# A shifted table of taps for the state-space stage: eight strided transfers, or one from a copy in DRAM

## The reference

```python
bu = einsum('blgc,gpc->blgp', u, bb)             # input to the states
s  = associative_scan(_complex_affine_combine, (a, bu), axis=1)
y  = einsum('blgp,gcp->blgc', s_re, c_re) - einsum('blgp,gcp->blgc', s_im, c_im) + d_skip * u
```

## Time and profile before

| | |
|---|---|
| median of 3 runs | 2849.48 us (2845.38 to 2862.76) |
| profiled execution | 2856.6 us, span of the core 2854.9 us |
| busy in the span | PE 92%, PEld 74%, DVE 72%, ACT 30%, POOL 12% |
| mean granted clock of TensorE | 0.959 of full speed |
| attention | 1285 to 1457 us |
| state stage | 1457 to 1612 us |
| traffic of the DMA queues | 480.96 MB, mean 168 GB/s |

### The profile page before, as it was taken

The page is one execution under the profiler, slowest core; times in us unless marked ns, Lnnn a source line. Parts: engine busy times, 40 slices in busy tenths (PEclk is TensorE's granted clock), DMA queues, the critical chain, the costliest instruction groups (busy, mean ns, idle before and its releaser), DMA issues. The chain is left out here.

```text
span 2854.9 us, 46052 instructions
## 1 busy us (share of the span) xinstructions
PE 2623.8 (92%) x15819; PEld 2118.9 (74%) x15819; DVE 2041.3 (72%) x2832; ACT 849.5 (30%) x1538; POOL 356.8 (12%) x588
## 2 busy tenths in 40 slices
PE   6779899999999999998867889998989999999998
PEld 3457666666666667884534679895879999999998
DVE  6549999988999956787871364528377777777767
ACT  4231112111122124008941452413233222222225
POOL 1010032323223220120012100024000000000000
PEclk8789999999999999999987999999999999999999
DMA  9876599989899963543258642126101111111121
GB/s 353 300 262 198 177 335 308 331 302 317 299 326 335 318 215 124 153 126 86 76 169 234 239 137 71 38 81 237 52 23 45 57 47 56 47 44 44 44 59 75
DMA packets 347829, 480.96 MB, mean 168 GB/s; under 512 B 31832, under 2 KB 229333, under 8 KB 345854
## 3 DMA queue, kind: packets, MB, share of 16 engines
q1 hardware_dynamic: 304742, 336.05, 36.2%
q0 software_dynamic: 42496, 142.33, 14.6%
q10 hardware_dynamic: 408, 0.31, 0.0%
HBM read 453.87 MB, written 22.62 MB: 167 GB/s over the span
## 5 line engine op out<-in xcount | busy, mean ns | idle before, releaser
L111 PE MATMUL banks<-ffn_ghi,whi 128*128 128x344 f32 (+1 forms) x880 | 318.2, 362 | 19.7 <-DVE xT L2250 10.4
L84 ACT ACTIVATE whi<-raw 128x1024 fp32r<-128x1024 f32 (+1 forms) x118 | 121.4, 1041 | 679.8 <-PE banks L113 587.6
L113 PE MATMUL banks<-ffn_ghi,wlo 128*128 128x344 f32 (+1 forms) x880 | 310.1, 352 | 0.0
L112 PE MATMUL banks<-ffn_glo,whi 128*128 128x344 f32 (+1 forms) x880 | 308.9, 351 | 0.0
L111 PE MATMUL banks<-a_hhi,whi 128*128 128x512 f32 x704 | 289.2, 411 | 6.9 <-DVE wlo L88 6.1
L624 DVE TENSOR_TENSOR ffn_kt<-ffn_kt,ffn_q 128x1024 f32<-128x1024 f32 x224 | 272.5, 1216 | 27.1 <-DMA ffn_kt<-in_cache_k_dram 27.1
L611 POOL DMA_DIRECT2D ffn_vt<-in_cache_v_dram x384 | 206.1, 537 | 663.6 <-issue 658.6
L112 PE MATMUL banks<-a_hlo,whi 128*128 128x512 f32 x704 | 279.2, 397 | 0.0
L113 PE MATMUL banks<-a_hhi,wlo 128*128 128x512 f32 x704 | 279.2, 397 | 0.0
L629 DVE TENSOR_REDUCE ffn_z<-ffn_kt 128x16 f32<-128x1024 f32 x224 | 272.5, 1217 | 5.7
L111 PEld LDWEIGHTS banks<-ffn_ghi,whi 128*128 128x128 f32 x880 | 166.3, 189 | 68.4 <-issue 23.3
(11 more groups left out here) (506 smaller groups left out, 5921.7 us busy)
## 6 DMA issues: line engine op xcount, KB each, us to landing
ffn_kt<-in_cache_k_dram SPq DMA_DIRECT2D x448, 256.0 KB, 4.4
ffn_vt<-in_cache_v_dram POOLq DMA_DIRECT2D x384, 256.0 KB, 5.1
raw<-in_w_ffn_gate_dram SPq DMA_DIRECT2D x44, 512.0 KB, 4.9
raw<-in_w_ffn_up_dram SPq DMA_DIRECT2D x44, 512.0 KB, 5.1
raw<-in_w_ffn_down_dram SPq DMA_DIRECT2D x44, 512.0 KB, 4.2
last_kt<-in_cache_k_dram POOLq DMA_DIRECT2D x64, 256.0 KB, 3.1
s_vt<-in_cache_v_dram SPq DMA_DIRECT2D x64, 256.0 KB, 6.0
s_vt<-in_cache_v_dram POOLq DMA_DIRECT2D x64, 256.0 KB, 5.8
```

The costliest lines, as they stand in the source:

```text
L84: act.activation(self.k.whi[c % W_RING][:, 0:self.width], self.slots[s][:, 0:self.width], ACT.Copy).then_inc(self.hi_done, 1)
L111: pe.matmul(out, whi, rhi, start=first, stop=False)
L112: pe.matmul(out, whi, rlo, start=False, stop=False)
L113: return pe.matmul(out, wlo, rhi, start=False, stop=last)
```

## The change

A second scratch tensor, `toep_scratch`, holds the shifted table as the state stage wants it: 128 rows of 32 x 128 floats, 16 KB each. During attention SP waits until the zeros have landed and then issues eight transfers from `kg_scratch` to `toep_scratch`, one for each row block. The state stage reads the table in one transfer of 2 MB, and SP's pages follow behind it without anything between. TensorE waits for 16 on `toep_in` in place of 128.

```diff
+        self.toep_dram = scratch("toep_scratch", [P, 32 * P])
...
+        self.toep_kept = self.sem("toep_kept")
...
                 sp.dma_start(self.kg_dram.rearrange("c (g a n) -> (c g) a n", g=8, a=4)[:, :, 0:P], zeros[:, :, :]).then_inc(self.zeros_kept, 16)
+                sp.wait_ge(self.zeros_kept, 16)
+                taps = self.kg_dram.rearrange("c (g n) -> c g n", g=32)
+                for l in range(8):
+                    sp.dma_start(self.toep_dram[16 * l:16 * l + 16, :].rearrange("c (g n) -> c g n", g=32),
+                                 taps[:, :, P - 16 * l:2 * P - 16 * l]).then_inc(self.toep_kept, 16)
                 for j in range(PAIRS):
...
-                sp.wait_ge(self.zeros_kept, 16)
-                taps = self.kg_dram.rearrange("c (g n) -> c g n", g=G)
-                others = late_v.OTHERS
-                for l in range(L):
-                    sp.dma_start(toep[l * C:(l + 1) * C, :, :], taps[:, :, P - l * C:2 * P - l * C]).then_inc(q["toep_in"], 16)
-                    late_v.load(sp, 1, others[4 * l:4 * l + 4])
-                late_v.load(sp, 1, others[4 * L:])
+                sp.wait_ge(self.toep_kept, 16 * L)
+                sp.dma_start(toep[:, :, :].rearrange("p g n -> p (g n)"), self.toep_dram).then_inc(q["toep_in"], 16)
+                late_v.load(sp, 1, late_v.OTHERS)
...
-                pe.wait_ge(q["toep_in"], 16 * L)
+                pe.wait_ge(q["toep_in"], 16)
```

## The result

| | before | changed |
|---|---|---|
| first comparison, median | 2852.89 us (4 runs) | 2822.18 us (4 runs), ratio 0.9895, interval 0.9852 to 0.9938 |
| second comparison, median | 2852.95 us (11 runs) | 2818.31 us (6 runs), ratio 0.9874, interval 0.9851 to 0.9897 |
| profiled execution, span | 2854.9 us | 2815.5 us |

The forecast was 2824 us, within a range of 2812 to 2842. By the two ratios the change makes the kernel 1.0 to 1.3% faster (30.7 and 34.6 us), and neither interval reaches 1.

A forecast was written before the change was run, and what follows sets the result against it. Stages between barriers bound the kernel: ScalarE in attention, TensorE's wait for taps in the state stage. State stage -28.8 us (24.8 earlier start, 4 clock), attention +3.3, sum -25.5 from 2849.5: 2824 us, range 2812 to 2842.

The forecast's parts named there:

- What ends the wait: State stage: the eighth transfer of taps, landing at 1520.7 us, ends TensorE's 16.82 us wait.
- When page 17 comes: State stage: page 17, now behind the whole table, lands at 1488.3 us, 1.5 us later than before.
- First product with taps: State stage: TensorE's products with taps follow the pages without a hole near 1496 us, 24.8 us earlier; bounds 19 to 27.
- The clock: State stage: products no longer begin behind a hole at low clock; 4 of 5.6 us lost come back, bounds 0 and 5.6.
- The price of the old pieces: State stage: the old taps moved at 89 GB/s, 23.5 us for the table, against 5.2 us in one transfer.
- Attention: Attention: zeros land at 1354 us, stores of pair 0 at 1371, so ScalarE loses 3.3 us waiting before pair 2.
- the eight copies: Attention: copies from DRAM to DRAM take 11 us, between 7.1 at the stores' rate and 23.5 at the taps'.
- (a): The forecast itself: state stage's gain and attention's loss about as predicted, net -12 to -28 us; chance 0.56.
- (b): Rival: copies in attention cost nothing and the clock comes back in full, -28.5 to -32 us; chance 0.23.
- (c): Rival: copies at the taps' 23.5 us or somewhat above stall attention 16 to 24 us, net -13 to -5; chance 0.12.
- (d): Rival: copies pay the taps' price on both sides, 47 us; ScalarE stands 39 us in attention, net +10; chance 0.06.
- (e): Rival: pages at 226 GB/s, not taps, hold TensorE in the state stage; gain 9 us, net -6; chance 0.03.

The follow-up runs named there:

- e7b: Changed kernel, table read in eight transfers of 128 partitions by 2 KB, pages between them as before; first product with taps 46.5 us after first gsum product.
- e6b: Changed kernel with the table's one transfer issued behind pages 17 to 31; first product with taps 38.2 us after first gsum product, then 31.2 us to the transposes.
- e4: Changed kernel with 24 copies in attention in place of 8; ScalarE's hole 13.10 us, attention 182.4 us against 168.8.
- e2: Changed kernel, table read from the DRAM copy in eight back-to-back transfers of 16 rows of 16 KB; first product with taps 52.7 us after first gsum product.
- e1: Kernel before, its eight transfers of taps back to back ahead of page 17, no DRAM copy; first product with taps 46.6 us after first gsum product.
- f3b: Same kernel as e1, profiled again and timed: first product with taps at 48.7 us; median 2836.55 us, ratio 0.9937 to before.
- e3: Changed kernel, DRAM copy laid out group by group, read in one transfer into 128 partitions; first product with taps 41.3 us after first gsum product.

## Why the prediction was right, point by point

**What ends the wait.** The eighth transfer's landing. Right: with the table earlier the hole is gone, and with only the order of before restored (e7b) it is back.

**When page 17 comes.** 8.5 MB at 400 GB/s, 30.3 us after SP's first issue. Measured 30.3 (1478.04 - 1447.72), at 413 GB/s. It is the new bound, and e6b shows that it is one of bytes.

**First product with taps.** Forecast 24.8 us earlier, measured 25.1 (63.6 - 38.5). A step inside was off: the last pages were to hold TensorE until 1494.7, which is 1484.4 in this execution. In the trace the thirty matmuls of pages 17 to 31 run in 7.46 us without a wait, at a granted clock of 0.50 up to 1483.5, while the DMA engines' flow ends at 1482.5. TensorE at the low clock was the last, not the pages. That the two lengths are alike is luck.

**The clock.** Forecast 4 of 5.6 us back; measured 31.55 - 26.80 = 4.75, give or take the spread of 1.9 us between kernels without a hole. e6b has the same term by itself, 4.4.

**The price of the old pieces.** 23.5 us for the table was too much: 14.7 and 17.3 when they stand together. The 226 GB/s of that stretch was put down to the taps' rate alone; what else there was in it stays open. The sum did not suffer, because it used only the new transfer's 5.2 us; but the part of the gain that needs no copy, 17 us, was not seen, and stands nowhere in the prediction.

**Attention.** Zeros landed at 1343.9, the forecast's 1354 less the 10.1 us by which this execution was ahead. The mis-sized term is the eight copies: 11 us forecast, 6.9 to 7.3 by e4. The last store of pair 0 landed at 1357.3 (1350.21 plus the 7.1 us of its landing) and not at 1361, and the hole of ScalarE is 0.24 us, not 3.3. The nearest row, the stores' 296 GB/s and 7.1 us, would have been right by itself. The 1.5 us to the first byte and the 1 us to the last receipt rest on no row of the prediction. In the DMA view the engines begin 1.3 us after the first copy's issue; the receipt was not measured. So by the marks (a) was the mechanism and (b) the amount: 29.8 us gained, 0.2 paid, against 28.8 and 3.3.

**The number.** The forecast gain was 25.5 us, the marks give 29.5, and the medians 30.7 and 34.6. That 2824 lies only 2 and 6 us above the two medians is in part luck: it was counted from 2849.5 us, and before measured 2852.9 in both comparisons.

**Rivals.** (c) and (d) fell by the copies' price, with their mechanism confirmed. (e) fell by the 413 GB/s. The copies' 286 to 304 GB/s is above what the prediction took from the Trainium skill for (c) and (d). In DMA: Bandwidth & Descriptors, "Latency and other measured facts", the Trainium skill gives 207 GB/s at a row pitch of 512 KiB and about half of it only at 4 MiB and more, so it says nothing of a loss at the 16 and 32 KB of these copies, and none shows.

## What to carry to other kernels

When a table arrives in pieces between other loads, look at both what each piece waits for and what each costs: the two multiply, and moving the pieces together may give most of the gain for nothing. Load to all 128 partitions at once, not 16 by 16: with rows of 16 KB that alone was 16.2 us for 2.1 MB. Look at the profile's packet counts before you say how small the pieces of a transfer were. A transfer put in front of stores that another engine waits for is free only as long as its length stays under that engine's slack, so double or triple it once to find the edge.

## What the runs showed of the hardware that was not expected

- 2.1 MB into 16 partitions at a time, estimated from when page 17 came: 98 GB/s in rows of 16 KB (e2), but 143 and 121 GB/s in pieces of 512 B (e1, f3b).
- A transfer that puts 512 B at a time into each of 128 partitions, from rows that are neighbours in DRAM, was recorded as 1024 packets of 2 KB (e3). Page 17 came 0.8 us later behind it than behind rows of 16 KB, but the issue next behind it on SP's queue took 16.57 us.
- Copies from DRAM to DRAM in 512 B pieces: 286 to 304 GB/s (e4).
- A hole of TensorE of 4.7 us costs about as much again behind it (4.4 us over the next 31 us). The granted clock was 0.50 in the first 10 us behind the hole, against 1.00 at the same place without it (e6b, changed kernel).
